# Feed-forward openings: the third weight slot's low part placed between the last sums, and the reload of an operand issued in two column parts

## The chip, the cores and the metric

The kernel runs on one core of a Trainium2 chip. The metric is the device time of one execution in microseconds (us). Five engines run their own queues of instructions and meet at semaphores: PE (TensorE, matmuls), DVE (VectorE), ACT (ScalarE), POOL (GpSimd) and SP (SyncE, which here only issues DMAs). All the transfers that this text speaks of are issued by SP on one hardware queue.

## What is computed

One inference step of a two-layer streaming encoder for 1024 prompt rows and 128 sample rows (1152 rows of width 1024, float32). Each layer is a mixer, an output projection and a feed-forward part. The change touches only where a layer's output projection gives way to its feed-forward part:

```python
for layer in range(DEPTH):
    ...
    x = x + mix @ w_out[layer]
    h = _rmsnorm(x, norm_ffn[layer])
    x = x + jnp.square(jax.nn.relu(h @ w_ff1[layer])) @ w_ff2[layer]
```

## The kernel before

**Precision.** A float32 value is split into a high part (ACT copies it to the format that PE reads) and a low part (POOL or DVE subtracts the high part from it). A product is three matmuls: high by high, high by low, low by high. Weights come by DMA into `raw`, ACT makes the high part in one of four slots of `split`, POOL the low part beside it (`low`, inside `mlp_pool_parts`, line 1336). The count `lo_ready` tells PE that a slot is whole.

**Feed-forward.** The product is done by a scheme of sums of quarters, which saves multiplications. The hidden columns go in 8 blocks of 512. In each block PE first makes hidden rows (`hidden_rows` in `mlp_pe`, line 987) by calls of `row_half` (24 matmuls of 288 columns, line 963), two calls for one weight slot and one operand. I call these pairs A to G:

| pair | weight slot | left operand in SBUF | holds |
|---|---|---|---|
| A | 0 | b21 = `operand(1, 0)` | MIXED |
| B | 1 | b12 = `operand(0, 1)` | UPPER1 |
| C | 2 | b11 = `operand(0, 0)` | normed rows |
| D | 3 | b21 | MIXED2, loaded over MIXED once A is done |
| E | 0 | b22 = `operand(1, 1)` | normed rows |
| F | 1 | b12 | UPPER3, loaded over UPPER1 |
| G | 2 | b21 | MIXED4, loaded over MIXED2 |

Then come the products with the second weights (`product`, line 1041). The five operands that don't stay in SBUF lie in DRAM (`operands[...]`), 2304 KB each: 128 partitions by 8 chunks (`m`) by 576 columns (`HALF`). In a steady block their loads are issued long before they are read.

**The opening.** The first block of each layer is different: the operands are only being made. The nine row tiles come out of the normalisation in the order `TAIL = (0, 4, 1, 5, 2, 6, 8, 3, 7)` and in groups `GROUPS = ((0, 1), (2, 3), (4, 5), (6, 6), (7, 8))`, positions in that order. Tiles 3 and 7 are the last group, number 4, and own columns 384 to 511; tile 8 (samples) owns columns 512 to 575. For each group DVE makes four sums (`c` = 0 to 3), ACT their high parts (line 696) and POOL their low parts (line 726), and SP stores them, each 512 KB in runs of 512 bytes (line 2058), to DRAM. Only then can a whole operand be loaded back (line 2040).

**Orders written out by hand.** POOL (`out_pool`): for each group the low parts of c = 1, 2, 0, 3; after the last group the low parts of weight slots 2, 3, 0, 1 and so on (`hidden_rows` of `mlp_pool`). SP (`mlp`, the loop over groups at line 2065): for the last group the store of MIXED, then, each after its low part, UPPER1 (c = 1) and MIXED2 (c = 2); then the load of MIXED2 into b21, which waits for every earlier store that it reads, and for pair A (`multiplied(0, 2)`); then the stores of UPPER3 (c = 0) and MIXED4 (c = 3). After them `inside(0)` goes on: the second weights' first quarter once slot 3's low part is made, then a wait for all stores of the last group, a quarter, the load of UPPER3, two quarters, and once pair D is done the load of MIXED4. DVE's first weight sum that touches slot 3's source (`weight_sums_of`, line 1419) waits for slot 3's low part, and DVE's adds of C's rows (line 1427), which D needs, stand behind it in DVE's queue.

## Time and profile before

| | us |
|---|---|
| median of 3 runs | 2767.18 |
| lowest, highest | 2763.03, 2767.97 |
| the profiled execution, its own time | 2760.91 |
| its span | 2759.1 |

The profiled execution lies 6.3 us below the median of the three runs. In its span PE is busy 2692.7 us. A row of the chain of waits or of the timeline starts with the start and the duration in us; "x48" counts instructions merged into the row; square brackets give the idle time just before it and what ended that. Times in the text are from the span's start. The opening of layer 0 lies at about 745 to 794 us, that of layer 1 at 2036 to 2086 us.

### The profile page before, as it was taken

What the parts mean: (1) busy time and instruction counts of PE and PEld (TensorE: products, weight loads), DVE (VectorE), ACT (ScalarE), POOL (GpSimd) and SP (SyncE); (2) the same over time, 40 slices, a digit from 0 to 9 for tenths busy, and PEclk for the clock granted to TensorE, in tenths of its full rate; (3) what the DMA queues carried; (4) which work ended last, traced back from release to release, by engine and by line L of the source; (5) the groups of instructions that cost most, each with busy time, mean ns of one, the idle gap of its engine ahead of it and who ended that gap; (6) DMA issues with size and microseconds to landing.
All of it is one profiled execution on the core that took longest, in us unless ns stands there. A gap on an engine that the chain in (4) does not pass through costs nothing.

```text
span 2759.1 us, 43942 instructions
## 1 busy us (share of the span) xinstructions
PE 2692.7 (98%) x17250; PEld 2469.9 (90%) x17250; DVE 1619.2 (59%) x2131; ACT 1056.5 (38%) x1713; POOL 1339.1 (49%) x764
## 2 busy tenths in 40 slices
PE   8999999999999999999999999999999999999998
PEld 8999987788889988999899989998888999889997
DVE  6943247683686677666743410198367766776665
ACT  6452347562533333333333301365243332333233
POOL 4343455343465555555632131287256555555552
PEclk9999999999999999999999999999999999999999
DMA  6477330244565444564433141024384654445541
GB/s 216 168 250 255 139 127 2 87 128 160 166 238 210 160 169 157 210 223 161 143 134 117 38 141 39 26 105 147 129 249 152 222 215 156 167 164 209 219 170 76
DMA packets 212593, 430.65 MB, mean 156 GB/s; under 512 B 27285, under 2 KB 153585, under 8 KB 201972
## 3 DMA queue, kind: packets, MB, share of 16 engines
q1 hardware_dynamic: 203840, 394.92, 40.9%
q0 software_dynamic: 7776, 31.24, 3.0%
q10 hardware_dynamic: 852, 2.75, 0.3%
q8 instruction: 88, 1.44, 0.2%
q14 instruction: 37, 0.30, 0.0%
HBM read 357.89 MB, written 70.94 MB: 155 GB/s over the span
## 4 chain that ended last, share of the span: by engine, by line
PE 82%; DVE 6%; issue 3%; POOL 3%; DMA 2%; ACT 2%; POOLq 1%; PEld 0%; DVEq 0%; PEldq 0%; ACTq 0%; SPq 0%
PE ps L963 24%; PE ps L1041 22%; PE ps L578 11%; PE ps L640 6%; PE ps L2575 5%; PE ps L588 4%; PE ps L1123 4%; DVE units L4215 1%; DMA units_r<-operands 1%; PE ps L2769 1%; POOL units_r L720 1%; DMA raw<-w_out 1%; DVE small L3949 1%; POOLq L311 1%; ACT ps L3656 0%
## 5 line engine op out<-in xcount | busy, mean ns | idle before, releaser
L1336 POOL TENSOR_TENSOR split<-raw,split 128x1024 fp32r<-128x1024 f32 x218 | 562.4, 2590 | 507.1 <-ACT split L1174 483.4
L963 PE MATMUL ps<-units_r,split 128*128 128x288 f32 x5376 | 718.8, 296 | 12.2 <-DMA units_r<-operands 5.7
L963 PEld LDWEIGHTS ps<-units_r,split 128*128 128x128 f32 x5376 | 715.7, 188 | 15.6 <-POOL split L1336 5.8
L1174 ACT ACTIVATE split<-raw 128x1024 fp32r<-128x1024 f32 x218 | 228.5, 1056 | 466.3 <-PE ps L963 177.5
L1451 DVE TENSOR_TENSOR units<-units,ps 128x512 f32<-128x512 f32 x434 | 285.0, 684 | 119.6 <-PE ps L1041 119.6
L578 PE MATMUL ps<-units_r,split 128*128 128x384 f32 x1872 | 328.9, 335 | 2.3 <-POOL split L291 1.5
L578 PEld LDWEIGHTS ps<-units_r,split 128*128 128x128 f32 x1872 | 324.4, 188 | 3.5 <-issue 1.7
L1041 PE MATMUL ps<-split,units_r 128*128 128x512 f32 x1344 | 309.8, 390 | 0.1
L1041 PEld LDWEIGHTS ps<-split,units_r 128*128 128x128 f32 x1344 | 252.3, 188 | 53.1 <-DVE units L1451 1.0
L1041 PE MATMUL ps<-split,spare_r 128*128 128x512 f32 x1008 | 235.7, 390 | 0.0
L1041 PEld LDWEIGHTS ps<-split,spare_r 128*128 128x128 f32 x1008 | 188.6, 188 | 38.4
L291 POOL TENSOR_TENSOR split<-raw,split 128x2048 fp32r<-128x2048 f32 x23 | 108.4, 4713 | 220.0 <-ACT split L286 219.4
L1427 DVE TENSOR_TENSOR units<-units,ps 128x576 f32<-128x576 f32 x96 | 72.3, 753 | 188.1 <-PE ps L963 188.1
L640 PE MATMUL ps<-split,units_r 128*128 128x512 f32 (+1 forms) x776 | 151.1, 354 | 6.3 <-DVE units_r L830 4.3
L640 PEld LDWEIGHTS ps<-split,units_r 128*128 128x128 f32 x776 | 128.2, 192 | 26.6 <-issue 5.1
L1184 ACT ACTIVATE units<-ps 128x576 f32<-128x576 f32 x128 | 83.2, 650 | 175.5 <-PE ps L963 175.4
L640 PE MATMUL ps<-units_r 128*128 128x512 f32 x632 | 150.1, 392 | 0.0
L1431 DVE SCALAR_TENSOR_TENSOR units<-units 128x576 f32<-128x576 f32 x96 | 145.6, 1557 | 0.0
L640 PEld LDWEIGHTS ps<-units_r 128*128 128x128 f32 x632 | 117.7, 188 | 23.8
L2575 PE MATMUL ps<-units_r,split 128*128 128x288 f32 x1008 | 134.0, 295 | 0.8 <-ACT units L3267 0.8
L2575 PEld LDWEIGHTS ps<-units_r,split 128*128 128x128 f32 x1008 | 133.7, 188 | 1.1 <-issue 1.0
L588 PE MATMUL ps<-split,units_r 128*128 128x256 f32 x864 | 106.5, 285 | 0.8 <-ACT units L3267 0.8
(536 smaller groups left out, 4032.9 us busy)
## 6 DMA issues: line engine op xcount, KB each, us to landing
units_r<-operands SPq DMA_DIRECT2D x76, 2304.0 KB, 8.8
raw<-w_ff SPq DMA_DIRECT2D x128, 512.0 KB, 4.4
units_r<-operands SPq DMA_DIRECT2D x22, 1152.0 KB, 7.4
raw<-w_in_even SPq DMA_DIRECT2D x14, 1024.0 KB, 9.3
raw<-w_in_odd SPq DMA_DIRECT2D x12, 1024.0 KB, 5.3
operands<-units_r SPq DMA_DIRECT2D x10, 1152.0 KB, 5.6
operands<-units_r SPq DMA_DIRECT2D x22, 512.0 KB, 3.9
operands<-split SPq DMA_DIRECT2D x18, 512.0 KB, 3.8
```

What stands on the lines that cost most here:

```text
L291: pool.tensor_tensor(split[:, n % 2, 1, :], raw[:, n % 2, :], split[:, n % 2, 0, :], ALU.subtract).then_inc(lo_ready, 1)
L578: last = pe.matmul(ps[:, bank + n, 0:GN], weights(slab, a, k, c0, P), h[b][:, k, n * GN:(n + 1) * GN], start=(k == 0 and q == 0), stop=(k ...
L588: last = pe.matmul(out, h[b][:, k, n * P:(n + 1) * P], weights(slab, a, k, 0, COLS), start=(k == 0 and q == 0), stop=(k == KC - 1 and q == 2))
L640: last = pe.matmul(out, tile_of(b, k, n), right[kind // 3][:, regions, a, COLS * k:COLS * k + COLS], start=(k == 0 and q == 0), stop=(k == ...
L963: last = pe.matmul(ps[:, bank + f, 0:HN], right_slot(base, slot, a)[:, COLS * k + P * f:COLS * k + P * (f + 1)], x[:, b, k, HN * g:HN * (g ...
L1041: last = pe.matmul(ps[:, bank, :], left(b, k), right_slot(base, (slot + 3) % 4, a)[:, 512 * k:512 * k + 512], start=(start and k == 0 and ...
L1123: one = pe.matmul(ps[:, bank, :], rows, weights(base + half, a, k, 0, 512, 512), start=(k == 0 and q == 0), stop=(k == HC - 1 and q == 2))
L1174: act.activation(right_slot(base, slot, 0), src, ACT.Copy).then_inc(hi_ready, 1)
L1336: pool.tensor_tensor(right_slot(base, slot, 1), src, right_slot(base, slot, 0), ALU.subtract).then_inc(lo_ready, 1)
L1431: dve.scalar_tensor_tensor(out=part_, in0=part_, scalar=0.0, in1=part_, op0=ALU.max, op1=ALU.mult).then_inc(ff_sq, 1)
L1451: dve.tensor_tensor(xx, xx, ps[:, bank, :], ALU.add).then_inc(ff_add, 1)
L2575: last = pe.matmul(ps[:, banks[g] + f, 0:HN], summed_slot(i, a)[:, COLS * k + P * f:COLS * k + P * (f + 1)], h[b][:, 4 * q + k, t], start= ...
```

## The change

1. POOL makes the low part of weight slot 2 (pair C's) between the low parts c = 2 and c = 0 of the last group, by a new helper `mlp_pool_third`; inside the loop over blocks the same instruction moves from a block's start to the end of the block ahead of it.
2. SP loads MIXED2 in two parts. Columns 0 to 383 (1536 KB, runs of 1536 bytes) are loaded behind the last group's store of MIXED and ahead of its stores of UPPER1 and MIXED2, and count on `c_out`. Columns 384 to 575 (768 KB, runs of 768 bytes) are loaded where the whole load stood, and count on `mixed_in`.
3. PE waits for `c_out` as well ahead of pair D; later waits on `c_out` count 16 more.

```diff
@@ out_pool
                 for c, high in ((1, 2), (2, 4), (0, 4), (3, 4)):
+                    if g == len(GROUPS) - 1 and c == 0:
+                        mlp_pool_third(pool, layer, base + 4, 0, 0)
                     pool.wait_ge(sums_hi, done + high)
@@ hidden_rows of mlp_pe
                 made(5)
+                pe.wait_ge(c_out, (32, 80)[layer])
                 mixed(1)
@@
+        def mlp_pool_third(pool, layer, base, blk, after):
+            low = mlp_pool_parts(pool, layer, base)
+            low(blk, 2, right_raw(base, 1, 1), 3 + HIGHS * after)
...
             def hidden_rows(blk):
-                low(blk, 2, right_raw(base, 1, 1), 3)
                 low(blk, 3, right_raw(base, 0, 0), 4)
...
                 mlp_pool_first(pool, layer, base, blk, 1)
+                mlp_pool_third(pool, layer, base, blk, 1)
@@ SP
+            FIRST_COLUMNS = tile_columns(TAIL[GROUPS[-1][0]]).start
+
+            def operand_columns(which, t):
+                return sp.dma_start(operand_rows(1, 0).rearrange("p (m t) -> p m t", t=HALF)[:, :, t],
+                                    operands[which].rearrange("p (m t) -> p m t", t=HALF)[:, :, t])
...
                     straight(MIXED, 1, 0, g)
+                    if g == len(GROUPS) - 1:
+                        sp.wait_ge(straight_out, STRAIGHT0 + 32 * len(GROUPS) * (layer + 1) - 16)
+                        sp.wait_ge(*stored_groups(layer, g - 1))
+                        sp.wait_ge(stored_groups(layer, g)[0], stored_groups(layer, g)[1] - 48)
+                        multiplied(0, 2)
+                        operand_columns(MIXED2, slice(0, FIRST_COLUMNS)).then_inc(c_out, 16)
                     for count, c in enumerate((1, 2, 0, 3)):
                         if g == len(GROUPS) - 1 and c == 0:
                             sp.wait_ge(straight_out, STRAIGHT0 + 32 * len(GROUPS) * (layer + 1))
                             sp.wait_ge(*stored_groups(layer, g - 1))
                             sp.wait_ge(stored_groups(layer, g)[0], stored_groups(layer, g)[1] - 32)
-                            multiplied(0, 2)
-                            operand_load(MIXED2)
+                            operand_columns(MIXED2, slice(FIRST_COLUMNS, HALF)).then_inc(mixed_in, 16)
```

POOL's queue around the last group in layer 0, before; `split<-raw` are weight slots 2, 3 and 0, `units_r<-units` of line 726 the low parts of the sums:

```order
161 L726 TENSOR_TENSOR units_r<-units,units_r 128x4x128 [waits fkT_taken]
162 L726 TENSOR_TENSOR units_r<-units,units_r 128x512 [waits fkT_taken] x3
163 L1391 UNCONDITIONAL_BRANCH
164 L1391 ISA
165 L1336 TENSOR_TENSOR split<-raw,split 128x1024 [waits hi_ready]
```

And after (lines are numbered anew there):

```order
161 L728 TENSOR_TENSOR units_r<-units,units_r 128x4x128 [waits fkT_taken]
162 L728 TENSOR_TENSOR units_r<-units,units_r 128x512 [waits fkT_taken]
163 L1339 TENSOR_TENSOR split<-raw,split 128x1024 [waits hi_ready]
164 L728 TENSOR_TENSOR units_r<-units,units_r 128x512 [waits fkT_taken] x2
165 L1398 UNCONDITIONAL_BRANCH
```

One slot's low part has moved ahead of two sums' low parts; the four instructions together are the same. Now SP's queue at the last group in layer 0, before; `straight_out` counts the stores of MIXED and UPPER1, `const_in` and `c_in` those of the other sums, `fkT_ready` is the count of sums' low parts, `ff_h` that of row halves:

```order
109 L2058 DMA operands<-units_r 1024x1x128 [waits par_ev]
110 L2058 DMA operands<-units_r 1024x1x128 [waits fkT_ready] x2
111 L2040 DMA units_r<-operands 128x4608 [waits const_in,ff_h,c_in,straight_out]
112 L2058 DMA operands<-units_r 1024x1x128 [waits fkT_ready] x2
113 L2027 DMA raw<-w_ff 128x2x512 [waits lo_ready]
114 L2027 DMA raw<-w_ff 128x2x512 [waits lo_ready,const_in]
115 L2040 DMA units_r<-operands 128x4608 [waits ff_h]
```

And after:

```order
109 L2071 DMA operands<-units_r 1024x1x128 [waits par_ev]
110 L2052 DMA units_r<-operands 128x8x384 [waits const_in,ff_h,c_in,straight_out]
111 L2071 DMA operands<-units_r 1024x1x128 [waits fkT_ready] x2
112 L2052 DMA units_r<-operands 128x8x192 [waits const_in,c_in,straight_out]
113 L2071 DMA operands<-units_r 1024x1x128 [waits fkT_ready] x2
114 L2034 DMA raw<-w_ff 128x2x512 [waits lo_ready]
115 L2034 DMA raw<-w_ff 128x2x512 [waits lo_ready,const_in]
116 L2047 DMA units_r<-operands 128x4608 [waits ff_h]
```

The first part of the load now stands ahead of the two stores (of UPPER1 and MIXED2) for which the second part waits, and carries a wait on stores of its own.

## Rows read from the trace of the kernel before

**Rows 1.** The page: engines' busy time; then a steady block in the chain of waits.

```profile
PE 2692.7 (98%) x17250; PEld 2469.9 (90%) x17250; DVE 1619.2 (59%) x2131; ACT 1056.5 (38%) x1713; POOL 1339.1 (49%) x764
...
1277.89 44.52 PE ps L963 x336
1322.41 43.54 PE ps L1041 x192
```

**Rows 2.** The timeline of PE, opening of layer 0, then of layer 1.

```profile
745.32 9.82 PE L963 MATMUL ps<-units_r,split 128*128 128x288 f32 x72
757.83 27.25 PE L963 MATMUL ps<-units_r,split 128*128 128x288 f32 x192 [2.68 <-POOL split L1336]
787.07 6.63 PE L963 MATMUL ps<-units_r,split 128*128 128x288 f32 x48 [1.99 <-DMA units_r<-operands]
...
2049.49 6.63 PE L963 MATMUL ps<-units_r,split 128*128 128x288 f32 x48 [2.67 <-POOL split L1336]
2057.82 12.98 PE L963 MATMUL ps<-units_r,split 128*128 128x288 f32 x96 [1.69 <-DMA units_r<-operands]
2071.39 6.62 PE L963 MATMUL ps<-units_r,split 128*128 128x288 f32 x48 [0.60 <-DMA units_r<-operands]
2079.44 6.62 PE L963 MATMUL ps<-units_r,split 128*128 128x288 f32 x48 [1.42 <-DMA units_r<-operands]
```

**Rows 3.** Layer 0, DMA issues, us to landing: issued 745.69, 752.02, 755.59, 755.99, 756.54.

```profile
operands<-units_r SPq DMA_DIRECT2D x1, 512.0 KB, 5.9
operands<-units_r SPq DMA_DIRECT2D x1, 512.0 KB, 3.4
units_r<-operands SPq DMA_DIRECT2D x1, 2304.0 KB, 9.9
operands<-units_r SPq DMA_DIRECT2D x1, 512.0 KB, 11.1
operands<-units_r SPq DMA_DIRECT2D x1, 512.0 KB, 12.0
```

**Rows 4.** By stretch: engines' busy us (count), PE clock, DMA share, GB/s; layer 0.

```profile
755.00:758.00 3.00, 0.32 (x3) 0.17 (x2) 0.00 (x0) 0.65 (x1) 3.00 (x3) 1.00 0.50 126
758.00:762.00 4.00, 4.00 (x20) 4.00 (x21) 1.78 (x1) 0.00 (x0) 4.00 (x2) 0.57 1.06 410
762.00:766.00 4.00, 4.00 (x33) 4.00 (x32) 2.18 (x2) 1.06 (x1) 1.67 (x2) 1.00 0.93 271
```

**Rows 5.** The timeline of POOL, layer 0, short stretches; then of DVE.

```profile
750.26 1.74 POOL L726 TENSOR_TENSOR units_r<-units,units_r 128x512 fp32r<-128x512 f32 x1 [0.50 <-ACT units_r L696]
751.95 2.28 POOL L726 TENSOR_TENSOR units_r<-units,units_r 128x512 fp32r<-128x512 f32 x1
...
755.43 7.00 POOL L1336 TENSOR_TENSOR split<-raw,split 128x1024 fp32r<-128x1024 f32 x3
...
750.87 2.21 DVE L1416 TENSOR_TENSOR raw<-raw 128x1024 f32<-128x1024 f32 x1
760.22 3.29 DVE L1419 TENSOR_TENSOR raw<-raw 128x1024 f32<-128x1024 f32 x1 [7.15 <-POOL split L1336]
763.44 0.74 DVE L1427 TENSOR_TENSOR units<-units,ps 128x576 f32<-128x576 f32 x1
2055.15 0.74 DVE L1427 TENSOR_TENSOR units<-units,ps 128x576 f32<-128x576 f32 x1
```

**Rows 6.** The timeline of SP, layer 0, short stretches.

```profile
749.78 0.51 SPq L2058 DMA_DIRECT2D operands<-units_r  x1
...
752.02 0.51 SPq L2058 DMA_DIRECT2D operands<-units_r  x1
...
768.96 0.49 SPq L2040 DMA_DIRECT2D units_r<-operands  x1
```

**Rows 7.** DMA issues elsewhere: 772.39; two together 235.12, 235.53; 2037.37; 2086.09.

```profile
units_r<-operands SPq DMA_DIRECT2D x1, 2304.0 KB, 14.6
units_r<-operands SPq DMA_DIRECT2D x1, 1152.0 KB, 5.6
units_r<-operands SPq DMA_DIRECT2D x1, 1152.0 KB, 8.7
operands<-units_r SPq DMA_DIRECT2D x1, 512.0 KB, 5.1
units_r<-operands SPq DMA_DIRECT2D x1, 2304.0 KB, 8.2
```

**Rows 8.** The chain of waits after pair F: layer 0, then layer 1.

```profile
808.74 3.47 PE ps L1041 x14
...
2079.50 2.97 DVE units L1431
...
2101.17 28.85 PE ps L1041 x126
```

More of the change, by code:

```diff
@@ L2149, in _ @@
                         at = slice(3 * g * D, (3 * g + 3) * D)
-                        sp.wait_ge(*((row_out[0], 64), (row_out[1], 32), (c_out, 48))[g])
+                        sp.wait_ge(*((row_out[0], 64), (row_out[1], 32), (c_out, 64))[g])
                         sp.dma_start(wide(6)[:, at], scratch[:, at]).then_inc(x_in[g], 16)
@@ L2527, in _ @@
                 pool.dma_start(o["y_prompt"][0, n * P:(n + 1) * P], unit(0, D, (n % 4) * D)).then_inc(slot_moved[n % 4], 16)
-            for stored, count in ((row_out[0], 64), (row_out[1], 32), (c_out, 48)):
+            for stored, count in ((row_out[0], 64), (row_out[1], 32), (c_out, 64)):
                 pool.wait_ge(stored, count)
```

## The prediction

> **What bounds the kernel now.** I read the page's busy times and the chain of waits first. PE is busy 2692.7 of 2759.1 us, and in a steady feed-forward block the chain is PE alone, 44.52 and 43.54 us with nothing between [rows 1]. So the change can matter only in the two openings. Next comes PE's timeline there [rows 2]. In layer 0 PE stands 2.68 us ahead of pair C, until POOL has made slot 2's low part, and 1.99 us ahead of G, until MIXED4 has landed. In layer 1 it is 2.67 us ahead of C, then 1.69, 0.60 and 1.42 us for the three loads ahead of D, F and G. The sum is 11.05 us, 0.4% of the time. That is all the change aims at. A pair without a wait takes 6.36 us (12.98 less 6.62) [rows 2].
>
> When does D start now? Layer 1: 2057.82. Layer 0's row runs from 757.83 to 785.08 over C, D, E and F; three pairs take 12.98 + 6.36 = 19.3 us, so D starts at about 765.8 [rows 2]. MIXED2, issued at 755.59, lands at 755.59 + 9.9 = 765.5 [rows 3], so there the load would have held PE too, had C not been slow: between 758 and 762 the granted clock is 0.57 (part of it at 1.2 instead of 2.4 GHz), with 20 matmuls in 4 us against 33 in the next 4 us [rows 4]. These 13 matmuls, at 0.13 us each, are 1.7 us; it came right after the stop ahead of C, and it costs only what the load doesn't hide.
>
> **Part 1: slot 2's low part ahead of two sums.** POOL's order was c = 1, 2, 0, 3, slot 2; the c = 2 piece ends at 750.26 + 1.74 = 752.0 and slot 2's piece starts at 755.43 [rows 5]. Moved, it starts at about 752.0. It takes 7.00 / 3 = 2.33 us alone; the piece that stands there now takes 2.28 us while DVE's own 2.21 us instruction runs beside it [rows 5], against 3.48 - 2.28 = 1.2 us for the next, so about 1.0 us is lost to DVE at that spot. I put slot 2's end at 755.3, where PE ends B (745.32 + 9.82 = 755.1 [rows 2]). C starts some 2.5 us earlier in each layer. Its first stop is gone.
>
> What is late next is D. It needs MIXED2 in SBUF, and DVE's add of C's rows. The add stands behind line 1419, which waits for slot 3's low part. POOL has the same pieces ahead of slot 3's end as before, so this end, the 3.29 us piece and the add (763.44 + 0.74 = 764.2; layer 1: 2055.15 + 0.74 = 2055.9) stay put [rows 5]. **D can't start before 764.2 and 2055.9**, 1.6 and 1.9 us earlier than now. Part 1 by itself is worth nothing: it moves PE's stop from ahead of C to ahead of D.
>
> The low parts c = 0 and 3 come 2.3 us later; their stores, before at 755.99 and 756.54, would wait for them, but part 2 holds them longer. In the loop over blocks the same move only crosses a branch, and PE has no wait there [rows 1]: nothing. The wait on `c_out` is one more for PE in each block, long satisfied after the first: nothing.
>
> **Part 2: the load in two.** This is where the sum is decided. SP now issues MIXED's store at 745.69, and stands until it has landed, 5.9 us later at 751.6 [rows 3]. Layer 1: 2037.37 + 5.1 = 2042.5 [rows 7]. Only then goes the first part. Behind SP's wait are queued the stores of UPPER1 and of MIXED2 (issued at 749.78 and 752.02 before [rows 6]), and those are what the second part waits for. On the one queue they come behind 1536 KB. That the queue serves in order the rows show: the stores issued 0.4 and 0.95 us after the whole load land at 767.1 and 768.5, after its 765.5, 1.6 and 1.4 us apart [rows 3].
>
> The price of the first part: the trace has no load with 1536-byte runs. Two loads of 1152 KB in 2304-byte runs, issued together on an idle queue, land after 5.6 us and 0.4 + 8.7 - 5.6 = 3.5 us later [rows 7], so 384 KB are 1.17 us. That gives 6.8 us for 1536 KB and 4.4 us for 768 KB. From below: the fastest whole load here takes 8.2 us [rows 7]; with 2.0 us fixed (a 512 KB store with next to nothing ahead of it takes 3.4 us, one in a row 1.4 [rows 3]) that is 6.1 and 4.1. From above: MIXED2's own 9.9 us with stores behind it [rows 3] gives 7.3 and 4.6. I take the middle, the rows with short runs.
>
> Layer 0, then: first part issued 751.7, landed 758.5; two stores behind it 1.6 + 1.4: 761.5; second part issued 761.6, landed **766.0**. Before: 765.5. D starts at about 766.1 instead of 765.8: 0.3 us later. The stores of UPPER3 and MIXED4 follow, landing 3.0 us later at 769.0, before 768.5. SP's loads of UPPER3 and MIXED4 stand behind these stores; from 768.5 to MIXED4's landing (772.39 + 14.6 = 787.0 [rows 7]) the queue is never short of work, so that lands 0.5 us later and G with it: **+0.5 us**.
>
> Layer 1: first part issued 2042.6, the stores landed at 2052.4, the second part at 2056.9; D at 2057.0 instead of 2057.82, -0.8. The stores behind land at 2059.9, before 2060.7 (2057.7 and 3.0 as in layer 0); UPPER3's load, and F, move by -0.8 with them. After F the chain goes through DVE, from 2079.50 to 2101.17 [rows 8], and starts with F's rows: it moves too: **-0.8 us**.
>
> The sum is -0.3 us, on 2760.91 of the profiled execution; on the median that is **2766.9**. Before, the queue was idle once between the stores and the load (DMA share 0.50 from 755 to 758 [rows 4]); now it is idle twice, once for each part, and that pays for the head start.
>
> The Trainium skill, DMA: Bandwidth & Descriptors, Anatomy of one DMA, gives a transfer about 2 us fixed plus its bytes at 436 GB/s. By it the first part would take 5.6 us, the second 3.8, and the sum would be about -4, the rival below. The rows above agree on the fixed 2 us; the whole load at 9.9 us is slower than its 7.4.
>
> **The rivals.** *The transfers pass quickly and both stops go* (18%). With 6.1 and 4.1 us and 1.4 a store the second part lands at 764.8 and 2055.7, the stores behind at 767.6 and 2058.5: -0.9 in layer 0; in layer 1 DVE's add bounds D (-1.9), F gains 2.2: about -3. With faster transfers still, DVE bounds both. From F's end (785.1; 2078.0) to the first piece held by DVE (808.74; 2101.17 [rows 8]) are 23.6 and 23.2 us, so layer 0 can gain 1.6 + 0.4, layer 1 1.9 + 0.6 for F, and G's 1.42 us is not paid out: the ceiling is -4.5. Taken: -3.8, **2763.4**. For it: little stands in the queue at 751.7. Against it: the 9.9 us of the whole load.
>
> *Slower: the gap ahead of D grows and the queue falls behind* (15%). If short runs go at MIXED2's rate or worse (7.3 and 4.6 us, 1.7 a store), the second part lands at 767.1 and 2058.0, the stores behind at 770.5 and 2061.4: +1.9 and +0.7 us. PE then idles 5 us ahead of D (761.7 to 767), longer than the 2.7 us after which the clock fell in layer 0 [rows 4]; another 1.7 us in each layer, hidden in layer 0 behind MIXED4 and open in layer 1 by about 1. Sum +3.6, **2770.8**. It decides from a second part landing later than 766.5, or 2057.7.
>
> *The first part doesn't start early*: slot 2's low part has its high part in time, and the columns of groups 0 to 2 are stored; I find nothing for it. It is within the 5% left.
>
> **How the numbers follow.** Forecast 62%, 2766.9, own range 2763.5 to 2769 (the prices' ends and the three runs' spread of 4.9 us). With both rivals and that spread the range is 2760 to 2771.5. A measurement can tell about 0.2%, 5.5 us, from no change. Even the ceiling is under it, and so is the slower rival; only runs' spread on top of a rival takes one over. Faster 0.07, same 0.85, slower 0.08.
>
> **What would show it.** In the profile after: C starts at about 755.4 and 2047.1; PE's stop now stands ahead of D, 4 to 5 us long, ended by the second part; SP issues the first part at about 751.7, UPPER1's store behind it; UPPER3's load at 769.4 (before 768.96 [rows 6]). It is wrong if D starts near 764.2, or if line 1419 starts earlier than 760.2, or if the median differs by over 5 us.

## The result, and the profile after

The changed kernel takes 2771.53 us (median of 15 runs, 2768.94 to 2777.51), the kernel before 2766.59 us (15 runs on the same chip, 2762.85 to 2770.01). The ratio is 1.0025, 95% interval 1.0018 to 1.0031, or 6.9 us: **slower**, by a little more than the bound of 0.2% named in the prediction. This ratio is not the quotient of the two medians, which lie 4.9 us apart; where a median and a ratio give different sizes below, the ratio with its interval decides. The predicted 2766.9 us lies below the measured median, and so, by a hair, does the whole range up to 2771.5.

The two profiled executions stand further apart than the medians: 2776.97 us after (near the slow end of its 15 runs), 2760.91 before (below the fastest of its 15). Their difference of 16.1 us can't be read as the change's price. So I measure each opening from its own first matmul of pair A. In layer 0 that stands at 743.13 after and 740.98 before, in layer 1 at 2044.03 and 2032.64. "Less 2.15" and "less 11.39" below put times of after on before's clock. The time from there to the first product of the second block grew by 6.4 us in layer 0 (141.0 to 147.4) and by 4.5 in layer 1 (141.7 to 146.2), 10.9 us in all.

The page of after, its busy times, and the group of pairs' matmuls. Its PE is busy 2701.4 us against 2692.7 [rows 1] with the same number of matmuls. Of the 15.8 us by which the span grew (2759.1 to 2774.9), PE spent 8.7 "busy": the same matmuls went more slowly.

```profile
PE 2701.4 (97%) x17250; PEld 2478.0 (89%) x17250; DVE 1622.2 (58%) x2131; ACT 1057.0 (38%) x1713; POOL 1339.4 (48%) x764
```

PE's timeline in the opening of layer 0, then of layer 1 (columns: start, us; in brackets the stop ahead of it and what ended it), to be laid beside [rows 2].

```profile
743.13 3.44 PE L965 MATMUL ps<-units_r,split 128*128 128x288 f32 x24 [0.51 <-DVE units L780]
...
757.54 6.63 PE L965 MATMUL ps<-units_r,split 128*128 128x288 f32 x48 [0.24 <-POOL split L1339]
770.38 21.14 PE L965 MATMUL ps<-units_r,split 128*128 128x288 f32 x144 [6.21 <-DMA units_r<-operands]
794.46 8.16 PE L965 MATMUL ps<-units_r,split 128*128 128x288 f32 x48 [2.94 <-DMA units_r<-operands]
...
2058.46 6.62 PE L965 MATMUL ps<-units_r,split 128*128 128x288 f32 x48 [0.27 <-POOL split L1339]
2070.94 21.09 PE L965 MATMUL ps<-units_r,split 128*128 128x288 f32 x144 [5.86 <-DMA units_r<-operands]
2094.16 8.17 PE L965 MATMUL ps<-units_r,split 128*128 128x288 f32 x48 [2.13 <-DVE units L1434]
```

C's stop is gone: 0.24 and 0.27 us where 2.68 and 2.67 stood. In its place stands a stop of 6.21 and 5.86 us ahead of D, ended by the load's second part. D starts at 770.38 less 2.15 = 768.2 (before 765.8) and at 2070.94 less 11.39 = 2059.6 (before 2057.82): 2.4 and 1.7 us late. Then two more things are slower than before. D, E and F take 21.14 and 21.09 us, against 19.3 at full speed. G takes 8.16 and 8.17 instead of 6.63.

The same stretches by windows say why (columns as in [rows 4]; the last but two is PE's granted clock as a share of 2.4 GHz). First C, the stop ahead of D and a piece of it, D's start and G in layer 0, then the stop and D's start in layer 1.

```profile
757.00:764.00 7.00, 6.76 (x51) 6.46 (x49) 1.55 (x1) 0.65 (x1) 7.00 (x5) 1.00 1.01 317
764.00:770.00 6.00, 0.17 (x2) 0.00 (x0) 6.00 (x5) 1.06 (x1) 3.61 (x2) 0.79 0.63 168
764.50:766.00 1.50, 0.00 (x0) 0.00 (x0) 1.50 (x2) 0.14 (x1) 0.16 (x1) 1.00 0.00 2
770.00:774.00 4.00, 3.62 (x15) 3.63 (x16) 1.50 (x2) 2.00 (x2) 1.85 (x1) 0.50 1.05 345
794.00:799.00 5.00, 4.54 (x23) 4.55 (x24) 5.00 (x2) 2.01 (x2) 4.92 (x3) 0.66 0.89 383
...
2065.00:2070.00 5.00, 0.08 (x1) 0.00 (x0) 5.00 (x5) 1.06 (x1) 2.67 (x2) 0.80 0.59 165
2070.00:2075.00 5.00, 4.06 (x17) 4.07 (x18) 2.87 (x2) 2.00 (x2) 3.15 (x2) 0.52 0.96 312
```

C now runs at 1.00, since nothing stops ahead of it. But the clock falls during the 6 us stop ahead of D, and D starts at 0.50 (1.2 GHz): 15 matmuls in 4 us, where 33 go at full speed [rows 4]. It falls once more at G (0.66). The stop's window also shows the queue half empty, 0.63 and 168 GB/s; from 764.5 to 766 it moved next to nothing (0.00).

The loads and stores that end D's stop, DMA issues of layer 0 (KB, us to landing), issued at 753.76 (first part), 754.39 (store of UPPER1), 764.62 (second part) and 778.82 (MIXED4), to be laid beside [rows 3, 7]; under them SP's timeline at the two parts.

```profile
units_r<-operands SPq DMA_DIRECT2D x1, 1536.0 KB, 7.7
operands<-units_r SPq DMA_DIRECT2D x1, 512.0 KB, 8.6
units_r<-operands SPq DMA_DIRECT2D x1, 768.0 KB, 5.6
units_r<-operands SPq DMA_DIRECT2D x1, 2304.0 KB, 15.5
```

```profile
753.76 0.58 SPq L2052 DMA_DIRECT2D units_r<-operands  x1
...
764.62 0.57 SPq L2052 DMA_DIRECT2D units_r<-operands  x1
```

And the chain of waits in both layers (start, us, what). It now runs through MIXED's store, SP, the store of MIXED2's last columns *behind* the first part, and then the second part.

```profile
747.85 5.90 DMA operands<-units_r
...
755.10 9.44 DMA operands<-units_r
...
764.62 5.63 DMA units_r<-operands
...
770.38 8.43 PE ps L965 x48
...
778.82 15.52 DMA units_r<-operands
...
2055.26 9.79 DMA operands<-units_r
...
2065.14 5.68 DMA units_r<-operands
```

The first part takes 7.7 us. The stores behind it land at 763.0 and 764.5, and only then does the second part go: 5.6 us more. Before, one issue of the whole load took 9.9 us [rows 3]; now 16.5 us lie from the first part's issue (753.76) to the landing of the second (770.26). The 4.0 us that the first part goes earlier (751.6 against 755.59) don't make up for these 6.6.

For POOL and DVE, short stretches of their timelines in layer 0, beside [rows 5]; the last two rows are DVE ahead of G in layer 1.

```profile
754.11 3.37 POOL L1339 TENSOR_TENSOR split<-raw,split 128x1024 fp32r<-128x1024 f32 x1
...
762.45 3.29 DVE L1426 TENSOR_TENSOR raw<-raw 128x1024 f32<-128x1024 f32 x1 [7.22 <-POOL split L1339]
...
2090.13 3.31 DVE L1467 TENSOR_TENSOR units<-units 128x1024 f32<-128x1024 f32 x1
2093.37 1.41 DVE L1434 TENSOR_TENSOR units<-units,ps 128x576 f32<-128x576 f32 x2
```

Slot 2's low part took 3.37 us (2.33 before, alone): it shares the stretch with DVE. DVE's 3.29 us piece starts at 762.45 less 2.15 = 760.3, before 760.22: slot 3's low part is where it was.

**The account.** Layer 0: D 2.4 us late; D to F 1.8 slower; 0.95 more stop ahead of G (2.94 against 1.99); G 1.5 slower: 6.7 in all, measured 6.4. Layer 1: D 1.7 late; D to F 1.8 slower, but before's 0.60 us stop ahead of F and what lay with it (0.9 in all) is gone; 0.7 more ahead of G, where DVE's add now stands queued behind a 3.31 us piece; G 1.5 slower: 4.8 in all, measured 4.5. Of these 11.5 us the four slow stretches (1.8 and 1.5 in each layer) are 6.6, and late data 4.9. The two shares are not independent: MIXED4's load is issued when D is done, so the slow D also makes that load later. Both numbers are of one profiled execution near the slow end of its spread; the 6.9 us of the ratio cover 15.

### The profile page after: what moved, and what is told of

The parts are those of the page before. It is cut to its first block, busy times and chain, and to the rows that moved or that the text cites. A ratio compares the mean times of both kernels' runs of the same rounds, so it can differ in the third digit from the quotient of the medians.

```text
span 2774.9 us, 43962 instructions
## 1 busy us (share of the span) xinstructions
PE 2701.4 (97%) x17250; PEld 2478.0 (89%) x17250; DVE 1622.2 (58%) x2131; ACT 1057.0 (38%) x1713; POOL 1339.4 (48%) x764
## 4 chain that ended last, share of the span: by engine, by line
PE 82%; DVE 6%; DMA 3%; issue 3%; POOL 3%; ACT 2%; POOLq 0%; SPq 0%; PEld 0%; PEldq 0%; DVEq 0%; ACTq 0%
PE ps L965 24%; PE ps L1044 22%; PE ps L578 11%; PE ps L640 6%; PE ps L2593 4%; PE ps L588 4%; PE ps L1126 4%; DVE units L4233 1%; DMA units_r<-operands 1%; PE ps L2787 1%; DMA operands<-units_r 1%; POOL units_r L720 1%; DMA raw<-w_out 1%; DMA raw<-w_in_even 1%; PE ps L3105 1%
## 5 line engine op out<-in xcount | busy, mean ns | idle before, releaser
L640 PEld LDWEIGHTS ps<-split,units_r 128*128 128x128 f32 x776 | 129.2, 193 | 26.5 <-issue 4.5
```

The source lines that it names most:

```text
L640: last = pe.matmul(out, tile_of(b, k, n), right[kind // 3][:, regions, a, COLS * k:COLS * k + COLS], start=(k == 0 and q == 0), stop=(k == ...
```

## The experiments

Every kernel below was timed in five rounds against the kernel before. Three batches of up to four kernels ran, each on one chip; before's medians there were 2764.40, 2765.52 and 2764.96 us. The theories were: **the order** (the first part in front of the stores empties the queue twice), **the cut** (short runs of columns are slow in themselves), **POOL's move** (the stop moved, and nothing is left), **the clock** (a long stop of PE costs speed besides), and **PE's wait** (D's first half row reads the first part alone, yet PE waits for the second).

| kernel | ratio to before (95%) | median us | opening, layer 0 / 1 |
|---|---|---|---|
| before | 1 | 2764.4 to 2766.6 | 141.0 / 141.7 |
| after | 1.0025 (1.0018 to 1.0031) | 2771.53 | 147.4 / 146.2 |
| e1, POOL's move alone | 1.0006 (0.9997 to 1.0015) | 2765.66 | 146.0 / 143.2 |
| e2, load in two alone | 1.0021 (1.0011 to 1.0030) | 2770.45 | 147.1 / 144.2 |
| e3, cut at the old place | 1.0001 (0.9992 to 1.0010) | 2765.47 | 141.5 / 142.3 |
| e4, e1 and SP's wait | 1.0013 (1.0004 to 1.0022) | 2768.16 | 144.2 / 144.1 |
| e5_peeled_only | 1.0024 (1.0013 to 1.0035) | 2773.40 | 146.2 / 146.5 |
| e5_stop_filled | 1.0017 (1.0008 to 1.0026) | 2771.00 | 143.9 / 143.8 |
| e7, second part waited for late | 1.0020 (1.0010 to 1.0029) | 2770.56 | 145.0 / 144.4 |
| e6, first part behind the stores | 0.9987 (0.9977 to 0.9996) | 2761.42 | 139.8 / 140.9 |
| e6_again | 0.9985 (0.9976 to 0.9994) | 2761.17 | 140.2 / 139.9 |
| e8, e6 and e7 | 0.9986 (0.9977 to 0.9995) | 2760.93 | 141.2 / 139.8 |
| e9, e8 and slot 3 earlier | 0.9988 (0.9979 to 0.9997) | 2763.32 | 140.2 / 141.5 |
| e10, e6 with POOL as before | 0.9985 (0.9976 to 0.9994) | 2760.81 | 139.8 / 140.4 |

"Opening" is, in the profiled execution, the time from A's first matmul to the first product of the second block.

### e1: POOL's move alone

The kernel before, with:

```diff
@@ out_pool
+                    if g == len(GROUPS) - 1 and c == 0:
+                        mlp_pool_third(pool, layer, base + 4, 0, 0)
@@ hidden_rows, summed_block of mlp_pool
-                low(blk, 2, right_raw(base, 1, 1), 3)
...
+                mlp_pool_third(pool, layer, base, blk, 1)
```

> Only POOL's part of the change: slot 2's low part between the last sums; SP's order and the whole load as before. Theory (the loss comes from the load in two: it lands late, and the clock falls in the long stop ahead of D): within 1.5 us of before; D starts where it did (about 20.5 us after B begins), PE's stop moves from ahead of C to ahead of D and is some 4 us long; it may cost a clock fall of up to 1.7 us in a layer. Rival (the moved piece collides with DVE, or lets PE run into longer stops): most of the 6.9 us, so +5 or more.

PE's timeline of e1 in layer 0, from A on:

```profile
746.63 3.42 PE L965 MATMUL ps<-units_r,split 128*128 128x288 f32 x24 [0.50 <-DVE units L780]
...
761.04 6.62 PE L965 MATMUL ps<-units_r,split 128*128 128x288 f32 x48 [0.25 <-POOL split L1338]
771.29 14.26 PE L965 MATMUL ps<-units_r,split 128*128 128x288 f32 x96 [3.63 <-DVE units L1437]
...
795.44 9.33 PE L965 MATMUL ps<-units_r,split 128*128 128x288 f32 x48 [2.91 <-DMA units_r<-operands]
```

C's stop is gone and D starts 24.66 us after A, before 24.8: the stop moved, as predicted. It is now longer than the one it replaces (3.63 us), D and E take 14.26 us instead of 12.98, and G is at 9.33 instead of 6.63: in this execution (2774.28 us, the slowest of e1's 11) the clock fell more than before. The median is 1.3 us over before's, and the ratio's interval holds 1. That its profile shows openings 5.0 and 1.4 us longer all the same is a warning on how far one execution can lie from the median.

### e2: the load in two alone

After, with POOL's order put back:

```diff
-                    if g == len(GROUPS) - 1 and c == 0:
-                        mlp_pool_third(pool, layer, base + 4, 0, 0)
...
             def hidden_rows(blk):
+                low(blk, 2, right_raw(base, 1, 1), 3)
...
-                mlp_pool_third(pool, layer, base, blk, 1)
```

> Only SP's and PE's part of the change: the load in two, its first part ahead of the last stores; POOL as before. Theory: +5 to +7 us, D as late as in the changed kernel (2.4 us late in layer 0, 1.7 in layer 1), with a stop of 2.7 us ahead of C and one of 3.5 to 4 us ahead of D. If two shorter stops keep the clock up better than one long one, +4. Rival (POOL's move is to blame): within 1 us of before.

PE's row at D in layer 0 (A at 743.13):

```profile
770.26 14.52 PE L963 MATMUL ps<-units_r,split 128*128 128x288 f32 x96 [2.12 <-DMA units_r<-operands]
```

D starts 27.1 us after A, as late as in after (27.3). The ratio is 1.0021, about 5.8 us over before: most of the loss sits in part 2 of the change by itself. Its interval (from 1.0011) begins just above the end of e3's (1.0010), which has the same cut at the old place.

### e3: the cut at the old place

The kernel before, with both parts issued one right after the other where the whole load stood:

```diff
+                pe.wait_ge(c_out, (32, 80)[layer])
                 mixed(1)
@@ SP
-                            operand_load(MIXED2)
+                            operand_columns(MIXED2, slice(0, FIRST_COLUMNS)).then_inc(c_out, 16)
+                            operand_columns(MIXED2, slice(FIRST_COLUMNS, HALF)).then_inc(mixed_in, 16)
```

> The load in two column parts, both issued where the whole load stood, one right after the other; POOL and the stores as before. It measures what cutting by columns costs, without the new order. Theory (the order is to blame: stores queued behind the first part, and the queue empty twice): the second part lands 0.5 to 1.5 us later than the whole load did, total +0.5 to +2. Rival (runs of 1536 and 768 bytes are slow): lands 3 us later or more, total +4 or more.

Its two issues in layer 0, at 758.22 and 758.85:

```profile
units_r<-operands SPq DMA_DIRECT2D x1, 1536.0 KB, 7.4
units_r<-operands SPq DMA_DIRECT2D x1, 768.0 KB, 9.0
```

The second lands at 758.85 + 9.0 = 767.9, 9.7 us after the first was issued; the whole load takes 9.9 us [rows 3]. I had expected it 0.5 to 1.5 us later than the whole load; it was 0.2 us earlier. The ratio is 1.0001. So runs of 1536 and 768 bytes cost nothing that these runs can tell, and the second part adds 2.2 us when it stands right behind the first. In the changed kernel, issued on a queue that has run empty, it took 5.6. The cut is refuted, and the order is left.

### e4: the wait alone

e1, with SP standing for the store of MIXED as in the changed kernel, but the load whole and at its old place:

```diff
                     straight(MIXED, 1, 0, g)
+                    if g == len(GROUPS) - 1:
+                        sp.wait_ge(straight_out, STRAIGHT0 + 32 * len(GROUPS) * (layer + 1) - 16)
```

> POOL's move, the whole load at its old place, and of the new order only SP's stand until MIXED's store of the last group has landed, ahead of the stores of UPPER1 and MIXED2. Theory: these stores land about 1 us later (in layer 0 UPPER1's is issued at 751.7 instead of 749.8), the load and D with them: +1 to +2 us in all over the POOL move alone. Rival (the stand itself is the loss): +5 or more over it.

PE's row at D in layer 0 (A at 739.85):

```profile
766.38 21.11 PE L965 MATMUL ps<-units_r,split 128*128 128x288 f32 x144 [5.49 <-DMA units_r<-operands]
```

1.0013, so 2.5 us over e1 by the medians, with intervals that overlap. The trace has it plainly: the stores of UPPER1 and MIXED2's last columns are issued later, behind the wait, and the load goes 16.1 us after A instead of 14.6. PE stops for 5.49 us ahead of D, and D starts 26.5 us after A (24.8 before, 27.3 in after); in layer 1 it is 26.4 (25.2 and 26.9). So SP's wait alone makes D late, before any part of a load stands there. In these traces it gives 1.7 of D's 2.4 us in layer 0 and 1.2 of 1.7 in layer 1: the larger share of D's lateness comes from the stores being issued later, the smaller from the bytes put in front of them and the second empty spell. What the wait costs in time over all runs is only suggested.

### e5: the stop filled

To weigh the clock, PE's first block of each layer is written out ahead of the loop. In e5_stop_filled C's second row half is computed three times in all in that block (48 matmuls more in each layer, about 6.4 us, in the stretch where PE would stand; the 12.7 us of the expectation are both layers together); e5_peeled_only has the block written out and nothing added, and is its measure.

```diff
                 row_half(pe, base, 2, b11, 0, SUM_BANKS[0])
+                for _ in range(again):
+                    row_half(pe, base, 2, b11, 1, SUM_BANKS[1], counts=False)
                 row_half(pe, base, 2, b11, 1, SUM_BANKS[1])
...
+            summed_block(0, 2)
-            with pe.Fori(0, LASTB) as blk:
+            with pe.Fori(1, LASTB) as blk:
```

> The changed kernel, with PE's stop ahead of D in each layer's first block filled: pair C's second half row is made three times (the same result; 48 matmuls more, 6.4 us). PE's first block stands ahead of the loop for this, so it is to be compared with the kernel that does that alone. Theory (the clock falls because PE stands still for 6 us): the granted clock stays at 2.4 GHz through D, D ends 1.7 us earlier in each layer, total 1.5 to 4 us below the peeled kernel, though PE does 12.7 us more work. Rival (the clock falls whatever PE does there, or the fall is hidden): the same time or above it.

> The changed kernel with PE's first block written out ahead of the loop, nothing else. A control: within 1 us of the changed kernel, so about +6 to +7 over before, with the clock falling as there.

PE's row from C on in layer 0, and the windows over the old stop and behind it: first e5_stop_filled, then e5_peeled_only.

```profile
757.86 32.18 PE L965 MATMUL ps<-units_r,split 128*128 128x288 f32 x240 [0.24 <-POOL split L1343]
...
758.00:770.00 12.00, 12.00 (x91) 12.00 (x92) 3.96 (x2) 1.37 (x2) 9.38 (x5) 1.00 0.81 237
770.00:774.00 4.00, 4.00 (x32) 3.96 (x31) 2.99 (x3) 1.06 (x1) 1.73 (x1) 1.00 1.04 341
```

```profile
769.38 22.02 PE L965 MATMUL ps<-units_r,split 128*128 128x288 f32 x144 [6.25 <-DMA units_r<-operands]
...
757.00:768.00 11.00, 6.12 (x47) 5.89 (x45) 6.56 (x5) 1.06 (x1) 8.67 (x5) 0.87 0.76 230
768.00:772.00 4.00, 2.62 (x11) 2.65 (x12) 1.54 (x1) 2.00 (x2) 1.80 (x2) 0.50 1.13 361
```

With the stop filled the clock stays at 1.00; without, it is 0.50 as D starts. Although it computes 48 matmuls more in each, the filled kernel's openings are 2.3 and 2.7 us shorter. So in these two traces the fall of the clock costs time on the path. Two cautions: the profile of e5_peeled_only (2777.76 us) is the slowest of its 8 runs, that of e5_stop_filled (2771.44) lies near its median; and in the medians the filled kernel is 2.4 us below its measure, but the intervals overlap. The size of the clock's price over all runs is not settled.

### e7: the second part waited for late

As e5_peeled_only, but in each layer's first block PE waits for the first part ahead of D's first row half, and for the second part only ahead of the half that reads it.

```diff
                 pe.wait_ge(c_out, (32, 80)[layer])
-                mixed(1)
+                if not first:
+                    mixed(1)
                 for g in range(2):
+                    if g and first:
+                        mixed(1)
```

> The changed kernel with PE's wait for the second part ahead of D's second half row only, in each layer's first block (D's first half row reads columns 0 to 287, all in the first part); the first block stands ahead of the loop. Theory: D's first half row starts at 764.2, when DVE's add is done (layer 0's times of before), the second waits for the second part at 768.1: D ends 3.2 us earlier than in the changed kernel, but MIXED4's landing holds G in layer 0 still, so 2 to 5 us less than the peeled kernel. Rival (the late landing of UPPER3 and MIXED4 sets the end, and D's start is free): the same time as the peeled kernel within 1 us.

PE's timeline in layer 0 (A at 743.12):

```profile
766.56 14.49 PE L965 MATMUL ps<-units_r,split 128*128 128x288 f32 x96 [2.39 <-DVE units L1441]
...
792.20 8.04 PE L965 MATMUL ps<-units_r,split 128*128 128x288 f32 x48 [2.61 <-issue]
```

D's first half starts 23.4 us after A, ended by DVE's add, as my bound had it (764.2 less A's 740.98 is 23.2). But the ratio is 1.0020, 2.8 us below its measure with overlapping intervals. The rest of the loss stays: G starts 49.1 us after A (46.1 before). The row gives no releaser ("issue"), but MIXED4's load, issued at 775.48, took 16.6 us and so landed at 792.1, 0.1 us ahead of G: it is late whether PE waits for the second part or not.

### e6 and e6_again: the first part behind the stores

After, with the first part moved behind the last group's stores of UPPER1 and MIXED2. It is issued when UPPER1's has landed, with MIXED2's still under way:

```diff
                     straight(MIXED, 1, 0, g)
-                    if g == len(GROUPS) - 1:
-                        sp.wait_ge(straight_out, STRAIGHT0 + 32 * len(GROUPS) * (layer + 1) - 16)
-                        sp.wait_ge(*stored_groups(layer, g - 1))
-                        sp.wait_ge(stored_groups(layer, g)[0], stored_groups(layer, g)[1] - 48)
-                        multiplied(0, 2)
-                        operand_columns(MIXED2, slice(0, FIRST_COLUMNS)).then_inc(c_out, 16)
...
                             stored(which, src, g).then_inc(stored_groups(layer, g)[0], 16)
+                        if g == len(GROUPS) - 1 and c == 2:
+                            sp.wait_ge(straight_out, STRAIGHT0 + 32 * len(GROUPS) * (layer + 1))
+                            multiplied(0, 2)
+                            operand_columns(MIXED2, slice(0, FIRST_COLUMNS)).then_inc(c_out, 16)
```

> The changed kernel with the first part issued behind the stores of UPPER1 and MIXED2 (once MIXED's and UPPER1's have landed, at about 753.3 in layer 0's times of before) instead of ahead of them; the second part as soon as MIXED2's store has landed (755.5). The column cut is the same. Theory (order and the empty queue are to blame): the second part lands at 764 to 765, so D starts 0 to 1.5 us earlier than before, total -3 to +1 against before. Rival (cutting by columns is to blame): as late as in the changed kernel, +5 or more.

> The version with the first part behind the stores once more, on the chip of the versions it is compared with. Expected 0.9977 to 0.9996 of before again, about -3.6 us.

e6's two issues in layer 0, at 754.44 and 756.97, and PE's timeline there (A at 742.17); then the window of D's start.

```profile
units_r<-operands SPq DMA_DIRECT2D x1, 1536.0 KB, 7.5
units_r<-operands SPq DMA_DIRECT2D x1, 768.0 KB, 7.2
```

```profile
756.59 6.62 PE L965 MATMUL ps<-units_r,split 128*128 128x288 f32 x48 [0.26 <-POOL split L1339]
765.51 20.87 PE L965 MATMUL ps<-units_r,split 128*128 128x288 f32 x144 [2.30 <-DVE units L1434]
786.83 6.63 PE L965 MATMUL ps<-units_r,split 128*128 128x288 f32 x48 [0.44 <-DVE units L1434]
...
764.00:770.00 6.00, 4.49 (x23) 4.49 (x24) 5.64 (x5) 2.43 (x3) 3.96 (x2) 0.73 1.05 346
```

The same cut, the same move of POOL, the same number of DMAs, and 0.9987 and 0.9985 instead of 1.0025: **3.6 us faster than before by the ratio, and by the two ratios some 10 us faster than after** (on its own chip, 9.1 us in the medians below e7, which has the change's order). That is a little more than the -3 to +1 that I had expected. The second part is issued 2.5 us behind the first, which it finds still under way, and lands at 764.2, 22.0 us after A (in after 770.26, 27.1). D is released by DVE at 23.3 us after A, where after has it at 27.3, and the queue is full while D runs (1.05). G's stop is 0.44 us. The clock still falls once, after D's 2.30 us stop (0.73).

Why it beats before as well: the first part goes 12.3 us after A, where the whole load went at 14.6, and what stands behind it moves up. UPPER3's load is issued 25.4 us after A (before 28.0), and MIXED4's, issued at 773.70, lands after 10.9 us, 42.4 us after A (before 46.0).

That the *place* in the queue is the cause of the loss is shown by this pair of kernels. The place brings two things at once, SP's stand ahead of two stores and 1536 KB in front of them; the pair doesn't part them, and e4 has only the first.

### e10: the same, with POOL as before

e6, with POOL's order of the kernel before (the edit of e2).

> The version with the first part behind the stores (e6: 0.9987 of before), with POOL's order as in the kernel before. Theory (POOL's move only shifts PE's stop from ahead of C to ahead of D, since D waits for DVE's add and the load): the same as e6 within 1.5 us, so -2 to -5 against before; C starts 2.7 us late, D without a stop of over 1 us. Rival (part of e6's gain is the moved low part): -1 or less against before. Rival on the other side (the move costs by itself, as the +1.7 of its own run may say): 1.5 us or more faster than e6.

PE's timeline in layer 0 (A at 741.25), and its row from C to G in layer 1:

```profile
758.10 27.25 PE L963 MATMUL ps<-units_r,split 128*128 128x288 f32 x192 [2.68 <-POOL split L1337]
785.93 6.63 PE L963 MATMUL ps<-units_r,split 128*128 128x288 f32 x48 [0.58 <-DVE units L1432]
...
2049.85 35.02 PE L963 MATMUL ps<-units_r,split 128*128 128x288 f32 x240 [2.70 <-POOL split L1337]
```

0.9985, the same as e6. The stop stands ahead of C again (2.68 us) and not ahead of D, at the same price: POOL's move is worth nothing here. Its median, 2760.81 us, is as low as any, with fewer edits. In layer 0 the row of C to F is the very one of before, 27.25 us [rows 2]; what is gained is G's stop, 1.99 before, 0.58 now. There the gain lies behind F, not ahead of D. In layer 1 the stops of before ahead of D, F and G (1.69, 0.60 and 1.42 us) are all gone: C to G are one row of 240 matmuls. It took 35.02 us instead of the 32.1 of full speed, with a granted 0.52 from 2049 to 2055.

### e8 and e9: what is left behind the load

e8 is e6 with the late wait of e7. e9 is e8 with slot 3's low part made early as well:

```diff
             low(blk, 2, right_raw(base, 1, 1), 3 + HIGHS * after)
+            low(blk, 3, right_raw(base, 0, 0), 4 + HIGHS * after)
...
             def hidden_rows(blk):
-                low(blk, 3, right_raw(base, 0, 0), 4)
```

> First part behind the stores, and PE's wait for the second part ahead of D's second half row only (PE's first block stands ahead of the loop). Theory: in e6 the second part lands before or just when DVE's add lets D start, so there is next to nothing left to gain: within 1 us of e6. Rival (the second part's landing still holds D): 1 to 3 us faster than e6.

> e8, and POOL makes slot 3's low part too ahead of the last group's c = 0 and 3 low parts, so that DVE's piece that waits for it, and the add of C's rows behind it, come about 2.5 us earlier. Theory: D's first half row can start at about 761.8 (layer 0's times of before), when the first part has landed; D to F end 1.5 to 2.5 us earlier, total 1 to 4 us below e6, if UPPER3 and MIXED4 land in time. Rival (the stores of c = 0 and 3, made 2.4 us later, hold up the queue and with it UPPER3 and MIXED4): the same as e6 or slower.

e8 has 0.9986: once DVE's add releases D, waiting later for the load gains nothing. e9 moves that add too. Its PE timeline in layer 0 (A at 742.28):

```profile
756.69 19.35 PE L965 MATMUL ps<-units_r,split 128*128 128x288 f32 x144 [0.25 <-POOL split L1346]
777.22 6.59 PE L965 MATMUL ps<-units_r,split 128*128 128x288 f32 x48 [1.18 <-issue]
786.44 8.15 PE L965 MATMUL ps<-units_r,split 128*128 128x288 f32 x48 [2.63 <-issue]
```

C, D and E run through without a stop, 144 matmuls in 19.35 us, and the kernel is no faster (0.9988). PE stops 1.18 us ahead of F and 2.63 ahead of G, and G runs slowly (8.15). G starts 44.2 us after A; in e6 it was 44.7. So the rival came: what PE gains at D it waits for at F and G. At G it is the same queue's later load that bounds it: MIXED4's, issued at 771.04, took 15.3 us and landed at 786.3, 0.1 us ahead of G. What released F the trace doesn't name.

## Why the prediction was wrong

**What was right.** C starts at 757.54 less 2.15 = 755.4 and 2058.46 less 11.39 = 2047.1, as written. The first part is issued at 751.6 and 2042.55 (751.7 and 2042.6). PE's stop moved to ahead of D and is ended by the second part, though it is 6 us long and not 4 to 5. The steady blocks are as before (44.52 and 43.5 us in the chain). Line 1426 (1419 before) starts where it did, so D can't start before DVE's add; e7 and e6 show that bound at work. "Part 1 by itself is worth nothing": e1's interval holds 1, and e10 equals e6. "Now it is idle twice" is true (DMA share 0.52 from 751 to 754 us, 0.00 from 764.5 to 766). It got a sentence, and too small a price. UPPER3's load, forecast at 769.4, went at 773.71 less 2.15 = 771.6. My sign "the median differs by over 5 us" would just have missed the loss, with medians 4.9 us apart; the ratio shows it.

**The step that failed first: the price of the two parts.** I took 6.8 and 4.4 us, the middle of my bounds, from two loads in longer runs issued together on an idle queue. Measured are 7.7 and 5.6 (8.1 and 5.7 in layer 1), all over my upper ends of 7.3 and 4.6. My upper ends scaled the whole load's 9.9 us by bytes, with 2.0 us fixed. e3 shows what was wrong with that: not the short runs, as the slower rival had it, since the cut costs nothing back to back (9.7 us for both). The second part alone, on an empty queue and with its own followers behind it, takes 5.6 us where in a row it adds 2.2. What was mis-sized is the fixed share. My 2.0 us came from 512 KB stores (3.4 less 1.4), and the two loads imply about as much (5.6 less 3.5); with e3's 2.2 us for each 768 KB, the whole load's 9.9 us leave 3.3 us fixed, and this estimate gives 7.7 and 5.5 for the two parts, as measured. How much of the 3.3 us is due to the DMAs queued behind isn't parted by any run.

The Trainium skill, DMA: Bandwidth & Descriptors, Anatomy of one DMA, has about 2 us fixed and the bytes at 436 GB/s, fitted there to DMAs issued by GpSimd; these are issued by SP. An estimate by it is 3.8 us for the second part; the trace, with 5.6, disagrees.

The sum of that term: the stores landed at 760.9 and 762.4, not both by 761.5. The second part went at 762.5, not 761.6, and landed at 768.1, not 766.0. In layer 1 it landed at 2059.4, not 2056.9. D came at +2.4 and +1.7 instead of +0.3 and -0.8. In layer 0 the two prices, 0.9 and 1.2 us too low, are the whole 2.1 us.

**The second: the clock.** I had seen that in layer 0 a 2.7 us stop was followed by a fall of the clock (in layer 1 the same stop, 2.67 us, was not: 1.00 from 2049 to 2053), and kept its 1.7 us for the slower rival, "hidden in layer 0 behind MIXED4 and open in layer 1 by about 1". The stop was 6 us, the clock fell in both layers, and it fell again at G, 1.8 and 1.5 us a time. Most of it was not hidden: in e5_peeled_only D to G took 2.7 and 3.6 us over full speed, and the filled kernel's openings are 2.3 and 2.7 us shorter. Even my forecast's own stop ahead of D, 4 to 5 us, should have carried that price; the forecast had it at nothing.

**The third: MIXED4.** From the landing of the last stores on I shifted everything by +0.5 us. That load was issued 4.3 us later than before (778.82 less 2.15 = 776.7, before 772.39), as its issue waits for D, and landed at 792.2, before 787.0: +5.2. "The queue is never short of work" was wrong as well: what can't be issued yet doesn't queue (DMA share 0.80 and 0.71 in the two stretches of 2 us ahead of 778, and in before 0.31 from 768.5 to 770). The chain of waits names it, from D's row to 778.82.

**The rivals and the chances.** The slower rival had most of the mechanism (a late second part, a longer stop, a fall of the clock) and a deciding point that held, a second part after 766.5 or 2057.7 (768.1 and 2059.4 came), but its sum of +3.6 was half of the 6.9. I gave "slower" 0.08, with the argument that each rival's time lies under the bound. The rival's parts had the same 2.0 us fixed, and this mistake sat in all three sums.

**What stays open.** How the 6.9 us of the ratio divide between late data and the clock isn't settled, nor how the late data divide between SP's stand and the 1536 KB in front of the stores (e4 says so for D's start alone): each profile is one execution, and those of before and after lie at opposite ends of their spreads. Some 5 us of the traces' 16.1 lie outside the openings, where the change does nothing (2.15 ahead of layer 0's A, most of the rest between the layers); no experiment was made on them. The differences e1 to before, e4 to e1, and e5_stop_filled or e7 to e5_peeled_only are not separated by their intervals.

## What to carry to other kernels

When a load is cut so that part of it can go early, look at what stands behind that part in the queue. If the rest of the load waits for those stores, the early part delays its own second half, and so does the wait that the issuing engine stands in for it: issue it behind them, while the queue is still full. Here that alone turned +6.9 into -3.6 us. Cost a cut by how often the queue runs empty, not by its bytes alone. And give a stop of PE of a few microseconds a price in clock, for the matmuls behind it and for the transfers that wait on them: the nine of 3.6 us or more ahead of D or F in these traces were all followed by slower matmuls, the shorter ones only in part.

## What the runs showed of the hardware

- Cutting a load by columns, down to runs of 768 bytes, cost nothing that shows back to back: 9.7 us for both parts, 9.9 for the whole, ratio 1.0001. The same 768 KB cost 5.6 us on a queue that had run empty.
- The clock: stops of 6.21 and 5.86 us were followed by a granted 0.50 and 0.52 over 4 and 5 us, a 2.30 us stop by 0.73 over 6. A second fall came at G after stops of 2.94 and 2.13 us, but not in before after 1.99 and 1.42 (G at 6.63 and 6.62 us there). The length alone doesn't decide for such short stops: before's 2.68 us in layer 0 was followed by 0.57, its 2.67 us in layer 1 by 1.00; e6_again's 2.31 us by 0.72, its 2.30 us by 1.00; e9's 1.80 us ahead of G in layer 1 by a slow G (8.14 us), its 3.25 us ahead of F there by a full-speed F (6.59 us). Repeated matmuls in the stop, whose results nobody uses, kept it at 1.00.
- DVE's piece of 128x1024 (line 1467, 1460 before) took 3.31 us in layer 1 of after, where it began inside a POOL instruction; 1.23 us in layer 1 of before, where POOL's next began 0.66 us behind it; and 3.31 us in layer 0 of before, again begun inside one. In layer 1 of after G waited for DVE's add, queued behind this piece.
